# Where the last query chunk of the first block is loaded, and in which order the expert sums change hands between phases

## The reference, cut to what matters

```python
q = (xb @ w_q).reshape(n, 8, 2, 128)               # 8 heads, two halves
s = einsum('nhie,ike->nhik', q, keys)              # 128 keys for each half
top_s, top_i = top_k(s, 16)                        # then the 16 best of the 16x16 sums
idx, gate = best 16 expert numbers per head, softmax of their scores
act = gelu(einsum('nhkd,nd->nhk', u[idx], xb))     # 128 experts a token
out = einsum('nhk,nhkd->nd', gate * act, v[idx])
h = h + out
```

## Time and profile before

| what | value |
|---|---|
| median of 3 runs | 1630.54 us (1628.32 to 1630.96) |
| profiled execution | 1629.12 us, of it 1627.3 us span |
| DVE / PE busy share of the span | 72% / 74% |
| DMA, mean over the span | 408 GB/s |
| granted TensorE clock, mean | 0.879 of full |

### The profile page before, as it was taken

The page is one execution under the profiler, slowest core; times in us unless marked ns, Lnnn a source line. Parts: engine busy times, 40 slices in busy tenths (PEclk is TensorE's granted clock), DMA queues, the critical chain, the costliest instruction groups (busy, mean ns, idle before and its releaser), DMA issues.

```text
span 1627.3 us, 21833 instructions
## 1 busy us (share of the span) xinstructions
PE 1202.7 (74%) x7488; PEld 591.0 (36%) x7488; DVE 1171.0 (72%) x3339; ACT 527.0 (32%) x1231; POOL 600.7 (37%) x542
## 2 busy tenths in 40 slices
PE   8876786868748887978687788799697855555565
PEld 3661232225415663533264355444234611111111
DVE  4479768668768687786677866788956886666665
ACT  0222143222224564642132355455311232222221
POOL 1034433533334244233333323441433345444442
PEclk9998897989879998998898799999798988777767
DMA  9879999999999999999999999999999989999997
GB/s 380 339 297 412 423 421 421 422 421 421 421 417 415 423 425 420 420 423 422 422 422 422 384 424 424 421 421 417 395 414 424 416 354 421 422 421 421 421 421 315
DMA packets 84079, 665.05 MB, mean 409 GB/s; under 512 B 9376, under 2 KB 9392, under 8 KB 11008
## 3 DMA queue, kind: packets, MB, share of 16 engines
q0 software_dynamic: 74752, 540.13, 80.3%
q1 hardware_dynamic: 9216, 123.53, 18.0%
HBM read 662.57 MB, written 1.05 MB: 408 GB/s over the span
## 4 chain that ended last, share of the span: by engine, by line
DMA 29%; PE 29%; DVE 26%; ACT 7%; issue 7%; POOL 2%; another core or an unknown queue 0%; DVEq 0%; POOLq 0%; ACTq 0%; SPq 0%
DMA ring<-in_experts,idx 28%; PE acc L928 11%; DVE ring L1584 9%; PE act_bank L610 7%; PE dve_bank L596 6%; DVE h L1390 2%; DVE onehot L1219 2%; DVE scratch L1219 2%; POOL ring L500 2%; ACT diag L1148 1%; ACT L990 1%; ACT h L1070 1%; PE act_bank L596 1%; ACT scratch L990 1%; PE act_bank L890 1%
## 5 line engine op out<-in xcount | busy, mean ns | idle before, releaser
L500 POOL DMA_INDIRECT ring<-in_experts,idx x510 | 573.5, 1125 | 947.6 <-PE acc L928 732.0
L928 PE MATMUL acc<-ring,diag 64*64 64x512 f32 x4080 | 608.2, 720 | 315.8 <-ACT diag L1148 307.9
L1584 DVE CUSTOM_DVE_ANT_0 ring<-ring,hn 128x1024 f32<-128x1024 f32 x512 | 620.7, 1224 | 220.1 <-DMA ring<-in_experts,idx 197.1
L928 PEld LDWEIGHTS acc<-ring,diag 64*64 64x64 f32 x4080 | 155.1, 153 | 665.2 <-ACT diag L1148 427.2
L1141 ACT ACTIVATE acts<-dots 128x2 f32<-128x2 f32 x256 | 52.1, 203 | 674.6 <-DVE dots L1584 642.2
L610 PE MATMUL act_bank<-hnT,wbuf 128*128 128x128 f32 x1728 | 218.0, 284 | 23.3 <-ACT h L1070 19.5
L1148 ACT ACTIVATE diag<-cst,coefs 128x64 f32<-128x64 f32 x512 | 150.3, 340 | 252.1 <-DVE coefs L1592 215.4
L610 PEld LDWEIGHTS act_bank<-hnT,wbuf 128*128 128x128 f32 x1728 | 205.2, 197 | 70.1 <-issue 63.0
L990 ACT ACT_TABLE_LOAD x80 | 102.6, 1283 | 19.4 <-DMA rowc<-in_rows 17.0
L1592 DVE TENSOR_TENSOR coefs<-acts,gate 128x2 f32<-128x2 f32 x256 | 42.7, 167 | 79.5 <-ACT acts L1141 64.7
L1141 ACT ACT_TABLE_LOAD x68 | 87.2, 1283 | 6.2 <-DVE dots L1584 0.3
(11 more groups left out here) (173 smaller groups left out, 1024.8 us busy)
## 6 DMA issues: line engine op xcount, KB each, us to landing
wbuf<-in_weights SPq DMA_DIRECT2D x48, 2048.0 KB
ring<-in_weights SPq DMA_DIRECT2D x7, 2048.0 KB, 19.4
ring<-in_experts,idx POOLq DMA_INDIRECT x510
kept<-in_weights SPq DMA_DIRECT2D x2, 2048.0 KB, 21.8
wbuf<-in_weights SPq DMA_DIRECT2D x2, 1024.0 KB, 7.0
scratch<-in_bias POOLq DMA_DIRECT2D x1, 1024.0 KB, 12.0
scratch<-in_bands POOLq DMA_DIRECT2D x1, 768.0 KB, 13.3
h<-in_x SPq DMA_DIRECT2D x1, 512.0 KB, 3.7
```

The source lines that it names most:

```text
L500: pool.indirect_dma_start(ring[:, n % RING], None, io[f"experts{layer}"], bass.IndirectOffsetOnAxis(idx[:, at:at + 1], 0),).then_inc(sem(f ...
L928: last[rows] = pe.matmul(acc[rows][half][home:home + HALF_P], diag[part, n % DIAGS], ring[part, slot, D + half * CW:D + (half + 1) * CW], ...
L1584: dve.tensor_tensor_reduce(out=ring[:, slot, 0:D], in0=ring[:, slot, 0:D], in1=hn[:, phase % NBLK], scale=1.0, scalar=0.0, op0=ALU.mult, o ...
```

## The change

Chunk 9 goes into the streaming buffer and is off the ring; the chunks behind it each move one place on in that buffer. The gain products stand ahead of head 0's queries. ScalarE does two heads' scores before the exponential of head 0, VectorE searches two heads ahead of slot 0 instead of three, and the parts of head 1's routing are due later (phase 0: at slots 4, 5, 6; later phases: parts 1 and 2 at slots 4 and 5 instead of 2 and 5). At a phase end VectorE copies the even halves into `h` without waiting for ScalarE (`copy_even`, behind slot 2), both engines tell after each half of the columns, and VectorE adds the odd sums one slot later (`add_odd`). TensorE's pair 0 starts the banks itself, half by half, and `take_stream` comes behind pair 2 and adds to the running sums.

```diff
@@ -53,7 +53,7 @@
 L1_CHUNKS = 8 + 4 + 4 + 4
 CHUNKS = (L0_CHUNKS, L1_CHUNKS)
 STAGED = RING // 2
-STAGED_AT = (5, 3, 0, 1, 2, 4, 5)
+STAGED_AT = (5, 3, 0, 1, 2, 4)
 LATE_CHUNK = 4
 
 
@@ -102,7 +102,7 @@
 START = [0]
 for _phase in range(PHASES):
     START.append(START[-1] + T_END[_phase // NBLK] + T_QUERIES)
-EARLY_HEADS, ROUTED_HEADS = 6, 3
+EARLY_HEADS, ROUTED_HEADS = 6, 2
 T_EARLY, T_ROUTED = (T_END0 + T_Q + T_PART * heads - 1 for heads in (EARLY_HEADS, ROUTED_HEADS))
 ASKED_FIRST, QUERIED_BY = 2, 14
 ASKED_BY = (121, 126)
@@ -125,6 +125,7 @@
      (98, T_OUT1 + 16 + OUT_LAG), (99, T_END1), (101, T_END1 + 1), (102.5, T_END1 + 2), (103.5, T_END1 + T_Q)),
 )
 FIRST_SIDE = GROUP + 2
+TAKEN_AT = 3 * GROUP + 1
 KNOTS = [(0, T_EARLY + 1), (ASKED_FIRST, START[1])]
 for _phase in range(1, PHASES):
     _from = (_phase - 1) * SLOTS + (QUERIED_BY if _phase == 1 else FIRST_SIDE)
@@ -136,6 +137,7 @@
 
 ROUTE_PARTS = 3
 ROUTE_LEAD, ROUTE_STEP = 17, 3
+ROUTE_FROM = 4
 ROUTE_DUE = []
 for _phase in range(PHASES):
     for _head in range(PH):
@@ -143,11 +145,13 @@
             _due = _phase * SLOTS + _head * TOPK - ROUTE_LEAD + _part * ROUTE_STEP
             if _head == 0:
                 _due = _phase * SLOTS - 15.5 + 1.5 * _part
-            ROUTE_DUE.append(max(_due, _part) if _head else _due)
-
-
-TOPS_FIRST = 3
-TOPS_DUE = [-3, -2, -2, 0, 1, 1, 3, 5]
+            if _head == 1 and (_part or not _phase):
+                _due = max(_due, _phase * SLOTS + ROUTE_FROM + (_part if not _phase else _part - 1))
+            ROUTE_DUE.append(_due)
+
+
+TOPS_FIRST = 2
+TOPS_DUE = [-3, -2, 0, 1, 2, 3, 4, 5]
 for _phase in range(1, PHASES):
     for _head in range(PH):
         _tick = START[_phase] + T_END[_phase // NBLK] + T_Q + T_PART * (_head + 1)
@@ -868,6 +872,13 @@
                 for half in range(2):
                     lane.need("h_ready")
                     transposes(h[:, b, half * CW:(half + 1) * CW], 4)
+                for half in range(2):
+                    out = fill("dve")
+                    for j in range(4):
+                        row = layer * KD + 4 * half + j
+                        ins = pe.matmul(out[:, j * P:(j + 1) * P], ident[:, row:row + 1].to_broadcast([P, P]),
+                                        gain_rows, start=True, stop=True)
+                    ins.then_inc(sem("dve_full"), 1)
 
                 for hd in range(PH):
                     at = base + T_Q + T_PART * hd
@@ -890,15 +901,6 @@
                         ins = pe.matmul(out[:, i * NK:(i + 1) * NK], qT[:, 2 * hd + i], keysT[:, layer, i],
                                         start=True, stop=True)
                     ins.then_inc(sem("act_full"), 1)
-                    if hd == 0:
-                        yield at + 3
-                        for half in range(2):
-                            out = fill("dve")
-                            for j in range(4):
-                                row = layer * KD + 4 * half + j
-                                ins = pe.matmul(out[:, j * P:(j + 1) * P], ident[:, row:row + 1].to_broadcast([P, P]),
-                                                gain_rows, start=True, stop=True)
-                            ins.then_inc(sem("dve_full"), 1)
 
             def side(layer, b):
                 yield from (mixer1 if layer else mixer0)(b)
@@ -911,7 +913,7 @@
                     for half in range(2):
                         ins = pe.matmul(acc[rows][half][part], folded[part],
                                         h[part, phase % NBLK, half * CW:(half + 1) * CW],
-                                        start=True, stop=False, skip_group_check=True)
+                                        start=False, stop=False, skip_group_check=True)
                     ins.then_inc(sem("stream_taken"), 1)
 
             def sum_pair(g, q, start=False, stop=False):
@@ -919,6 +921,9 @@
                 pe.wait_ge(sem("diag_ready"), g * GROUPS + (q + 1))
                 last = [None, None]
                 for half in range(2):
+                    if start and g:
+                        pe.wait_ge(sem("even_copied"), 2 * (g // STEPS - 1) + half + 1)
+                        pe.wait_ge(sem("odd_copied"), 2 * (g // STEPS - 1) + half + 1)
                     for odd in range(GROUP):
                         n = q * GROUP + odd
                         slot = (g * BODY + n) % RING
@@ -927,7 +932,7 @@
                             home = (rows ^ odd) * HALF_P
                             last[rows] = pe.matmul(acc[rows][half][home:home + HALF_P], diag[part, n % DIAGS],
                                                    ring[part, slot, D + half * CW:D + (half + 1) * CW],
-                                                   start=start and odd == 1, stop=stop, skip_group_check=True)
+                                                   start=start, stop=stop, skip_group_check=True)
                 for rows in range(2):
                     last[rows].then_inc(sem(f"pairs_summed{rows}"), 1)
 
@@ -956,17 +961,14 @@
             def experts(phase, beside):
                 first = phase * STEPS * GROUPS
                 for n in range(SLOTS + GROUP):
-                    if n == GROUP:
-                        if phase:
-                            pe.wait_ge(sem("acc_read"), phase)
-                            pe.wait_ge(sem("odd_copied"), phase)
-                        take_stream(phase)
                     if n >= GROUP and n % GROUP == GROUP - 1:
                         at = n // GROUP - 1
                         if first + at == PHASES * STEPS * GROUPS - 1:
                             sum_last_pair()
                         else:
                             sum_pair((first + at) // GROUPS, at % GROUPS, start=at == 0, stop=at == SLOTS // GROUP - 1)
+                    if n == TAKEN_AT:
+                        take_stream(phase)
                     if n < SLOTS:
                         beside.upto(pace(phase, n))
 
@@ -1159,8 +1161,8 @@
                         home = slice((1 - rows) * HALF_P, (2 - rows) * HALF_P)
                         started = lane.start(act.activation(odd_sums[part, half * CW:(half + 1) * CW],
                                                             acc[rows][half][home], ACT.Copy))
-                lane.after(started)
-                lane.tell("odd_copied")
+                    lane.after(started)
+                    lane.tell("odd_copied")
 
             def move_last_odd():
 
@@ -1592,19 +1594,23 @@
                 dve.tensor_tensor(coefs[:, cols], acts[:, cols], gate[:, bass.ds(at, GROUP)],
                                   ALU.mult).then_inc(sem("coef_done"), 1)
 
-            def read_acc(phase):
+            def copy_even(phase):
 
                 for rows in range(2):
                     dve.wait_ge(sem(f"pairs_summed{rows}"), (phase + 1) * STEPS * GROUPS + AHEAD)
-                lane.need("odd_copied")
                 for half in range(2):
                     for rows in range(2):
                         part = slice(rows * HALF_P, (rows + 1) * HALF_P)
                         cols = slice(half * CW, (half + 1) * CW)
-                        started = lane.start(dve.tensor_tensor(h[part, phase % NBLK, cols], odd_sums[part, cols],
-                                                               acc[rows][half][part], ALU.add))
-                lane.after(started)
-                lane.tell("acc_read")
+                        started = lane.start(dve.tensor_copy(h[part, phase % NBLK, cols], acc[rows][half][part]))
+                    lane.after(started)
+                    lane.tell("even_copied")
+
+            def add_odd(phase):
+
+                for half in range(2):
+                    lane.need("odd_copied")
+                tt(h[:, phase % NBLK], h[:, phase % NBLK], odd_sums, ALU.add)
 
             def move_last_even():
 
@@ -1630,7 +1636,9 @@
                     g = first + n // BODY
                     dot(phase, g, n % BODY)
                     if n == GROUP and phase:
-                        read_acc(phase - 1)
+                        copy_even(phase - 1)
+                    if n == GROUP + 1 and phase:
+                        add_odd(phase - 1)
                         if phase == PHASES - 1:
                             lane.tell("out_ready")
                     if n >= FIRST_SIDE or not phase:
```

## The result

| | before | changed |
|---|---|---|
| median, 20 runs each | 1629.45 us (1627.59 to 1631.96) | 1632.01 us (1630.04 to 1634.3) |
| ratio | | 1.0015, 95% interval 1.0009 to 1.0021 |
| profiled execution, its span | 1629.12, 1627.3 us | 1630.04, 1628.2 us (the fastest of its twenty) |

The kernel became 2.5 us slower; 1624.3 was forecast, and 1632.01 lies outside the range. It lies in the class "within 0.2%", which had 0.16. Twenty runs a side told the two apart at 0.15%, so that class was wider than what can be measured.

A forecast was written before the change was run, and what follows sets the result against it. DMA transfers were taken as the bound. Start -1.5, phase 1 end -0.1, phase 0 end -0.2 and phase 2 end -4.4 sum to -6.2 us: 1622.9 for the profiled execution, 1624.3 for the median; range 1619.5 to 1629.5.

The forecast's parts named there:

- pair 0 ends at 1317.8 ... its gather 1318.7: End of phase 2: pair 0 ends at 1317.8 instead of 1322.9, its gather issues at 1318.7 instead of 1323.76.
- the hole behind pair 0 closes: End of phase 2: engines run dry at 1320.3, so a gather at 1318.7, with 1.4 us to data, leaves no gap.
- idle time is length times (1 - share): Pricing rule for all DMA dips: stretch length times missing mean share, 24.6 us over four stretches.
- what is saved in one place reaches the end undiminished: Whole kernel: removed DMA idle time shortens the run fully, as long as the engines stay full behind it.
- -4.4 us at phase 2: End of phase 2: of 5.2 us idle, 0.8 stays, so 4.4 us is gained; bounds -5.2 to -1.5.
- the first rival: Phase ends: the hole moves behind four early gathers, before pair 2's; total -3.5 us, 1627; chance 20%.
- 1328.4 at full clock: End of phase 2: pair 2 runs from 1325.6 to 1327.6 at 2.4 GHz and its gather issues at 1328.4.
- the first stretch: Start, 72.5 to 87: idle 13.05 us, to grow by 5.0 for chunk 11 and shrink by 1.6 at head 0.
- the second rival: Start: TensorE's clock stays low at head 0, +0.1 for -1.6; total -4.5 us, 1626; chance 8%.
- one VectorE search moves ... and head 1's routing to slots 4 to 6 ... That hides it: nothing.: Start: moved VectorE work costs nothing, since slots 12 to 15 give ten more us of transfers before slot 16.
- The third rival: Start: chunk 11 is displaced and the second idle stretch stays, slot 12 late; total +3.4 us, 1634; chance 8%.
- the dip that it closes: Start, 112.5 to 134: slot 10 waits, 4.9 us idle, taken as wholly gone; bounds -4.9 to 0.

The follow-up runs named there:

- start alone: Only the start part (chunk 9, gain products, searches, phase 0 routing) put into the kernel before, old phase ends: 1631.55 us, ratio 1.0014.
- start with late searches: Kernel before with the start part, searches of heads 6 and 7 due at slots 7 and 9, old phase ends: 1628.56 us, ratio 0.9991.
- the same, chunk in the ring: Kernel before with the start part and searches of heads 6 and 7 later, but chunk 9 left in the ring, old phase ends: 1629.03 us, ratio 0.9991.
- phase end alone: Only the phase-end part (copies by halves, residual rows, head 1's later routing) put into the kernel before, old start: 1628.82 us, ratio 0.9998.
- late searches, new phase ends: Changed kernel with searches of heads 6 and 7 due at slots 7 and 9 instead of 4 and 5: 1628.41 us, ratio 0.9994.
- ring chunk, new phase ends: Kernel before with gain products first, two heads searched ahead, later searches, new phase ends, chunk 9 left in the ring: 1627.86 us, ratio 0.9986.
- k = 4: Kernel before with GpSimd's gather of slot 64 in each phase made to wait for four more pairs: +30.1 us, ratio 1.0189.

## Why the prediction was wrong

**The phase end: the dip closed, and one engine had never been idle in it.** Step "pair 0 ends at 1317.8 ... its gather 1318.7": 1316.9 and 1317.78. Step "the hole behind pair 0 closes": it did. The step that failed is the sum behind it, "idle time is length times (1 - share)", with "what is saved in one place reaches the end undiminished": -4.4 us at phase 2, -4.7 with the other phase ends, where -0.3 +- 1.5 was measured. The windows of the kernel before show why, the dip and then the last transfers of the kernel:

```profile
1321.00:1325.00 4.00, 3.16 (x28) 0.99 (x26) 3.51 (x8) 0.79 (x3) 1.24 (x1) 0.99 0.06 27
...
1614.00:1616.00 2.00, 0.00 (x0) 0.00 (x0) 1.34 (x4) 0.20 (x1) 0.00 (x0) 1.00 0.82 332
1616.00:1618.00 2.00, 1.27 (x12) 0.51 (x16) 2.00 (x4) 0.59 (x2) 0.00 (x0) 1.00 0.17 70
1618.00:1620.00 2.00, 1.76 (x12) 0.30 (x8) 1.15 (x4) 1.37 (x4) 0.00 (x0) 0.50 0.03 10
```

A share of 0.06 is one engine in 16, and 27 GB/s is a sixteenth of 417: through those 4 us one engine worked on alone, on transfers of which the other 15 had finished their parts, and when it was done the next data were there. The trace's single packets agree: from 1321.3 to 1325.5 they stand one behind the other, 309 ns for each of 8 KB (gathers) and 159 ns for each of 4 KB (weights).

The trace also notes, for each gather, when each engine signals that its part has landed: 16 marks a gather, where none is missing. In the kernel before, the last gather to land ahead of the dip has 15 marks by 1320.28 and the sixteenth at 1327.20, 6.9 us later; behind the dip the sixteenth is 1.3 us late or less in the gathers up to 1345. In the changed kernel it stays late: 15 marks by 1331.44 and the sixteenth at 1336.14, for instance, and VectorE's dot, which waits for this gather, starts at 1336.16. A gather counts as landed when its slowest engine is done. Two dots of the changed kernel:

```profile
1336.16 1.28 DVE L1586 CUSTOM_DVE_ANT_0 ring<-ring,hn 128x1024 f32<-128x1024 f32 x1 [0.65 <-DMA ring<-in_experts,idx]
...
1339.01 1.23 DVE L1586 CUSTOM_DVE_ANT_0 ring<-ring,hn 128x1024 f32<-128x1024 f32 x1 [1.55 <-DMA ring<-in_experts,idx]
```

The dip was the other 15 waiting. Close it, and they go on ahead; the slowest gains next to nothing. The tail shows that it is so. The last windows of the changed kernel:

```profile
1612.00:1614.00 2.00, 0.30 (x4) 0.30 (x8) 0.93 (x4) 0.79 (x3) 0.00 (x0) 0.91 0.44 178
1614.00:1616.00 2.00, 2.00 (x12) 0.49 (x9) 1.06 (x2) 0.00 (x0) 0.00 (x0) 0.50 0.09 39
1616.00:1618.00 2.00, 1.28 (x8) 0.00 (x0) 1.43 (x4) 0.20 (x1) 0.00 (x0) 0.74 0.06 25
1618.00:1620.00 2.00, 1.36 (x16) 0.51 (x16) 2.00 (x3) 0.59 (x2) 0.00 (x0) 1.00 0.08 31
1620.00:1622.00 2.00, 1.23 (x16) 0.36 (x12) 1.63 (x5) 1.43 (x5) 0.00 (x0) 1.00 0.03 10
```

And the marks of the last gather to land, in the four pairs of kernels that differ in the phase ends alone (old ends / new ends; one execution each, and executions of one kernel differ by some us):

| pair | 8 of 16 marks by, us | 15 by | the sixteenth |
|---|---|---|---|
| start alone / changed | 1618.0 / 1613.2 | 1619.0 / 1615.6 | 1622.0 / 1621.3 |
| start with late searches | 1614.1 / 1610.4 | 1614.8 / 1611.4 | 1619.7 / 1618.9 |
| the same, chunk in the ring | 1615.4 / 1610.0 | 1616.6 / 1610.8 | 1619.5 / 1618.5 |
| before / phase end alone | 1616.6 / 1615.8 | 1618.2 / 1617.0 | 1619.4 / 1622.3 |

In the first three pairs most engines are through 3.7 to 5.4 us earlier with the new ends, and the slowest 0.8 to 1.1. The fourth shows no gain for the slowest either, but its second execution was the slowest of its kernel (1631.03 against a median of 1628.82). The same for all in another measure: what is still to move when a slot's gather is issued (bytes of the windows behind it, less 1.05 MB for each gather still to come, at 420 GB/s), and the time from slot 509's issue until the last engine stops:

| kernel | in flight at slot 400, us | at slot 509, us | slot 509 until the last engine stops, us |
|---|---|---|---|
| before | 8.4 | 16.9 | 26.3 |
| start alone | 8.4 | 16.0 | 26.5 |
| changed | 4.0 | 12.9 | 27.2 |
| phase end alone | 4.5 | 14.3 | 27.1 |
| late searches, new phase ends | 3.9 | 11.6 | 26.3 |
| ring chunk, new phase ends | 4.8 | 11.5 | 26.2 |

At slot 400 the new phase ends have 4 us less in flight, the very 4.4 us that I booked. With 2 to 5 us less in flight at slot 509 the last transfer ends no sooner. So the term was near 0.

Gathers go out no earlier either: slot 400 at 1329.85 against 1329.59. For this one the reason is the first rival's and not a late landing. Its pair 2 comes behind head 1's numbers in VectorE's list (TensorE idle 5.05 us until 1325.31) and then takes 3.69 us for 16 products, at a granted clock of 0.50 (1325 to 1329), against 1.95 us before. My step for it, 1328.4 at full clock, was 1.4 us early:

```profile
1325.31 3.69 PE L933 MATMUL acc<-ring,diag 64*64 64x512 f32 x16 [5.05 <-ACT diag L1150]
```

From 1336 on the dots wait for landings, as shown above. Four pairs of kernels differ in the phase ends alone, and by their ratios these are worth -0.3 us (alone), +0.2 (changed against start alone), +0.5 (with late searches) and -0.8 (chunk in the ring), each +- 1.5 or more, -0.1 on average; -4.7 was booked. One smaller part is not separated: summed over an execution, the packets of the same bytes took 0.1 to 3.6 us longer (mean of the 16 engines) with the new ends than in their twins.

Why the slowest engine falls behind, and which it is, stays open: neither packets nor marks name their engine. The gaps agree with a lag that mostly grows from one common stop to the next. In the kernel before, the last stop ahead of the phase 2 dip was at 117 us, and the share is under 0.15 for 4.5 us of the dip. With gaps made ahead of it, it has only 1.5 us of that. Here it is in the kernel with k = 4, all of it (the sixteenth mark is 2.4 us late ahead of it):

```profile
1348.00:1352.50 4.50, 3.41 (x28) 0.87 (x28) 4.40 (x11) 1.36 (x5) 2.50 (x2) 1.00 0.40 121
```

**The start.** Right: the first stretch (+3.4 forecast, +3.5 measured), head 0's 32 products in 3.84 us at a granted clock of 1.00 instead of 5.47 (so the second rival falls), slot 0's gather at 83.16 (83.4), slot 10 right behind slot 9, slot 12 at 114.36 (110.5 to 115), the dip at 112.5 to 118 gone. Here are the gain products in the old idle time and head 0's behind them, to set against the earlier trace rows:

```profile
65.44 1.95 PE L879 MATMUL dve_bank<-cst 128*128 128x128 f32 x16
67.44 3.84 PE L614 MATMUL act_bank<-hnT,ring 128*128 128x128 f32 x32
```

Wrong, and the reason that the kernel became slower instead of staying the same: "one VectorE search moves ... and head 1's routing to slots 4 to 6 ... That hides it: nothing." I checked slot 16 against ten us of transfers in flight, but not against VectorE's list ahead of pair 2, where 5 us of searches and 6.5 of routing now stood together, behind a stall of ScalarE. It cost 3.6 us of dip, and the searches alone, moved away, gave 3.4 us back. The third rival named "searches that now stand between dots" as its cause, and gave it a price of the right size, but put it on slot 12; it was slot 16.
By parts, from the ratios: chunk +1.5, gain products -1.5, the order of searches and routing +2.3 (what the whole start leaves over, not timed by itself), phase ends -0.3: +2.0 of the 2.5 us, each +- 1.5. My start was -1.5 where +2.3 was measured. I had the chunk at +5.0 and the dip that it closes at -4.9.

**The first rival at the end of phase 1** came as forecast (0.77 before from 905 to 911): the hole moved, from 905 to 911 to a smaller one at 915 to 919 (share 0.88) and one at 926 to 931 (0.91). One slip in the chances: half of the first rival's 0.20 is 0.10, and the sum of 0.78 counts it as 0.07.

## What to carry to other kernels

Before you price a dip in the DMA share, look at how deep it is: at 0 all engines stop and it costs what it shows; at 1/16 one engine is still working and may set every landing, and then closing the dip only lets the others run ahead. Compare the last landing signal of a gather with the one before it. Don't test a price for idle time by the mean idle time of a whole execution: with the same bytes it follows the time by itself. When work is moved out of one gap, follow the moved work to its new place and add up that engine's list there, in front of the next thing that frees a buffer, even where the transfers in flight seem to cover it.

## What the runs showed of the hardware

- Under full load one DMA engine of 16 falls behind the others. In the kernel before, the sixteenth mark of a gather comes 0.1 us behind the fifteenth at 121 us, 1.9 at 481, 3.3 at 649 and 5.7 at 1309; it doesn't grow evenly, and single gathers have more (7.6 at 519). In the last gather it is 1.2 us late there and up to 7.6 in the others. Behind a dip in which the 15 wait for it, the lag is 1.3 us or less (kernel before, 1320 to 1325). At k = 4 the share lies under 0.15 for 3.5 us between 667 and 678.5, and for 1 us in the next dip, which begins 6 us behind the first.
- A share near 1 isn't full rate: from 1320 to 1327 the changed kernel shows 0.96 at 329 GB/s, against 1.01 at 420 between 86 and 112.5. Read the GB/s beside the share.
- ScalarE waits of 5 to 7 us that end on a cause the profile calls remote stand in both kernels once the gathers fill the engines: 5.63 us until 92.25 and 6.80 until 94.76. What they are wasn't tried.
